# One sequence of 48 units for the cross-attention of a decoder trunk, with the cached keys and values asked for in ScalarE's DMA queue

## What is computed

```python
x = x + einsum('bte,ed->btd', o, w_out)                       # mixer's output
# memory of the prompt: 256 tokens
m = rmsnorm(mem_prompt, g_mem)
k = einsum('bmd,de->bme', m, w_k)        # also an output (new_mem_k_prompt)
v = einsum('bmd,de->bme', m, w_v)        # also an output (new_mem_v_prompt)
# cross attention: 4 heads of 512; prompt uses k, v above, the 8 samples use
# cache_mem_k, cache_mem_v: (1, 8, 256, 4, 512) each, 16.8 MB each
q = einsum('btd,de->bte', rmsnorm(x, g_xattn), w_q)
p = softmax(q k^T * 512**-0.5)
x = x + einsum('btd,de->btd', p v, w_o)
# then SwiGLU with D_FF = 5632 and a last RMSNorm
```

## Time and profile before

| | |
|---|---|
| median of 3 runs | 2031.25 us (2029.52 to 2032.12) |
| the profiled execution, its own time | 2029.23 us |
| its span, first to last instruction | 2027.5 us |
| PE busy over the span | 1868.7 us (92%) |
| DVE, ACT, POOL busy | 1158.9, 763.5, 243.3 us |
| mean granted TensorE clock | 0.969 |
| transferred | 362.42 MB, mean 179 GB/s |

### The profile page before, as it was taken

The page is one execution under the profiler, slowest core; times in us unless marked ns, Lnnn a source line. Parts: engine busy times, 40 slices in busy tenths (PEclk is TensorE's granted clock), DMA queues, the critical chain, the costliest instruction groups (busy, mean ns, idle before and its releaser), DMA issues.

```text
span 2027.5 us, 34488 instructions
## 1 busy us (share of the span) xinstructions
PE 1868.7 (92%) x13799; PEld 1749.6 (86%) x13799; DVE 1158.9 (57%) x1590; ACT 763.5 (38%) x768; POOL 243.3 (12%) x225
## 2 busy tenths in 40 slices
PE   4999999858695999999988999999999999999996
PEld 3999999755694989977764898999999999999996
DVE  5788445473834655555556565666544466665444
ACT  1454554322224343333333234444333344443332
POOL 6000000001711540000000351000000000000331
PEclk9999999889897999999999999999999999999998
DMA  5455555700032545677867366898745789895552
GB/s 158 153 179 166 168 169 186 225 3 11 1 94 84 180 152 168 227 265 265 319 211 274 96 184 184 256 253 238 197 143 172 207 234 246 242 252 148 171 175 95
DMA packets 407132, 362.42 MB, mean 179 GB/s; under 512 B 10975, under 2 KB 373470, under 8 KB 404214
## 3 DMA queue, kind: packets, MB, share of 16 engines
q1 hardware_dynamic: 379686, 336.53, 53.9%
q10 hardware_dynamic: 27392, 25.17, 3.9%
HBM read 345.67 MB, written 16.19 MB: 178 GB/s over the span
## 4 chain that ended last, share of the span: by engine, by line
PE 84%; DVE 8%; issue 3%; ACT 2%; POOL 1%; DMA 1%; DVEq 0%; POOLq 0%; ACTq 0%; SPq 0%
PE ps L419 64%; PE ps L439 9%; PE ps L831 2%; DVE w_lo L403 2%; PE ps L1158 1%; PE ps L1148 1%; PE ps L947 1%; DMA vc<-in_cache_mem_v_dram 1%; PE ps L1047 1%; PE ps L1112 1%; ACT w_hi L396 1%; PE ps L999 1%; DVE cacc L519 0%; DVE Tm L1853 0%; DMA raw<-in_ffn_w_up_dram 0%
## 5 line engine op out<-in xcount | busy, mean ns | idle before, releaser
L396 ACT ACTIVATE w_hi<-raw 128x2048 fp32r<-128x2048 f32 (+1 forms) x289 | 519.9, 1799 | 924.9 <-PE ps L419 784.4
L403 DVE TENSOR_TENSOR w_lo<-raw,w_hi 128x2048 fp32r<-128x2048 f32 (+1 forms) x289 | 629.6, 2179 | 273.4 <-ACT w_hi L396 269.3
L419 PE MATMUL ps<-act_hi,w_lo 128*128 128x264 f32 x2576 | 740.0, 287 | 3.6 <-DVE w_lo L403 1.9
L419 PE MATMUL ps<-act_lo,w_hi 128*128 128x264 f32 x2576 | 732.3, 284 | 0.0
L419 PE MATMUL ps<-act_hi,w_hi 128*128 128x264 f32 x2576 | 731.8, 284 | 0.0
L419 PEld LDWEIGHTS ps<-act_hi,w_lo 128*128 128x128 f32 x2576 | 487.9, 189 | 6.9 <-DVE w_lo L403 6.2
L419 PEld LDWEIGHTS ps<-act_lo,w_hi 128*128 128x128 f32 x2576 | 488.2, 190 | 0.7
L419 PEld LDWEIGHTS ps<-act_hi,w_hi 128*128 128x128 f32 x2576 | 485.5, 188 | 0.0
L419 PE MATMUL ps<-ff_hi,w_lo 128*128 128x264 f32 x704 | 202.0, 287 | 4.3 <-DVE ff_lo L542 4.3
L419 PE MATMUL ps<-ff_hi,w_hi 128*128 128x264 f32 x704 | 201.4, 286 | 0.0
L419 PE MATMUL ps<-ff_lo,w_hi 128*128 128x264 f32 x704 | 200.9, 285 | 0.0
(11 more groups left out here) (365 smaller groups left out, 1944.2 us busy)
## 6 DMA issues: line engine op xcount, KB each, us to landing
raw<-in_w_in_dram SPq DMA_DIRECT2D x56, 1024.0 KB, 6.8
raw<-in_ffn_w_gate_dram SPq DMA_DIRECT2D x44, 1024.0 KB, 5.8
raw<-in_ffn_w_up_dram SPq DMA_DIRECT2D x44, 1024.0 KB, 10.5
raw<-in_ffn_w_down_dram SPq DMA_DIRECT2D x32, 768.0 KB, 4.8
raw<-in_ffn_w_down_dram SPq DMA_DIRECT2D x32, 640.0 KB, 6.1
raw<-in_w_out_dram SPq DMA_DIRECT2D x16, 1024.0 KB, 6.7
raw<-in_xa_w_q_dram SPq DMA_DIRECT2D x16, 1024.0 KB, 6.7
raw<-in_xa_w_k_dram SPq DMA_DIRECT2D x16, 1024.0 KB, 6.3
```

What stands on the lines that cost most here:

```text
L396: act.activation(w_part(ph, w_hi[b]), raw_part(ph, r, half), ACT.Copy)\
L403: dve.tensor_tensor(w_part(ph, w_lo[b]), raw_part(ph, r, half), w_part(ph, w_hi[b]), ALU.subtract)\
L419: mm = pe.matmul(ps[:, acc(ph, u), 0:ph.cols], w[b][:, k, :], v[:, kk + k, 0:ph.cols], start=first and k == 0 and m == 0, stop=last and k ...
```

## The change

All 48 units of `x_q`, `mem_k` and `mem_v` become one written-out sequence, n = 0 to 47, and the attention's steps are placed between units:

- The query is turned per head (after units 4, 10, 18, 26), and `spread_query` and `sample_scores` run from unit 5 to 36, head by head instead of sample by sample.
- Keys are turned after units 20, 24, 28, 32; the prompt's scores come after 22, 26, 30, 34, its shares are turned after 23, 27, 31, 35; the samples' softmax at 37 and 38.
- Sample values 0 to 15 come after units 40 to 47, two each. Values 16 to 31 and all 16 prompt tiles come after unit 47, one prompt tile and one sample value in turn.
- Keys and values come in 64 pieces of 512 KB, asked for by ScalarE (`piece_in`, line 1527 of the kernel after): the first 14 through three buffers in the room of the turned keys, the others through a ring of eight in the room of `x_q`'s operands. SyncE keeps the weight slots and the results.

```diff
-            for n in range(NB):
-                ph = PH["mem_k" if n < 4 else "mem_v"]
-                load(sp, ph, n % 4, 0)
-                if n:
-                    key_turn(n - 1, 2)
-                    key_turn(n - 1, 3)
...
+            for s in range(3):
+                load_slot(s)
+            for m in range(3 * KT):
+                if m % 2 == 1 and m < 46:
+                    load_slot((m + 5) // 2)
+                if m >= 20 and m % 4 == 0:
+                    rows_out((m - 20) // 4)
...
+            def piece_in(p):
+                if p < EARLY_PIECES:
+                    if p >= EARLY:
+                        W(act, "s_dot", p - EARLY + 1 + 2)
+                elif p < EARLY_PIECES + RING:
+                    act.wait_ge(units_done, PH["mem_k"].u0 + UNIT_CREDIT)
+                elif p < NB * XH + RING:
+                    W(act, "s_dot", p - RING + 1 + 2)
+                else:
+                    W(act, "s_o", p - RING - NB * XH + 1)
...
+                act.dma_start(dst[:, :, :], part.rearrange("(m p) d -> p m d", p=P)).then_inc(landed, 16)
...
+            for n in range(3 * KT):
+                split(*unit_at(n + 2))
+                m = n - 1
+                if 5 <= m < KT and nxt < EARLY_PIECES or KT <= m < 37 or m >= 40:
+                    piece_in(nxt)
+                    nxt += 1
+                    if m >= 40 or 22 <= m <= 30 and m % 2 == 0:
+                        piece_in(nxt)
+                        nxt += 1
...
+                if n >= KT and n % 4 == 3:
+                    keep_rows(n % KT // 4, n // (2 * KT))
...
+                if n >= 39:
+                    for v in range(2):
+                        first_values(2 * (n - 39) + v)
+            for v in range(18, NB * XH):
+                first_values(v)
+                if v % 2 == 1 and nxt < PIECES:
+                    piece_in(nxt)
+                    piece_in(nxt + 1)
+                    nxt += 2
```

More of the change, by code:

```diff
@@ L441, in wide_products, with piece_at, unit_at @@
             mm.then_inc(units_done, 1)
+        def piece_at(p):
+            if p < EARLY_PIECES:
+                return early[p % EARLY], ring_landed[RING - 1 - p % EARLY], 16 * (p // EARLY + 1)
+            n = p - EARLY_PIECES
+            used = len(range(RING - 1 - n % RING, EARLY_PIECES, EARLY)) if n % RING >= RING - EARLY else 0
+            return ring[n % RING], ring_landed[n % RING], 16 * (used + n // RING + 1)
+        def unit_at(m):
+            ph = PH[("x_q", "mem_k", "mem_v", "x_o")[m // KT]]
+            return ph, m % KT // 4, m % 4
         def acc(ph, u):
@@ L653, in _, with load_slot @@
             rest("w_out", True)
[L654 to L670, removed]
+            def load_slot(s):
+                ph, i, u = unit_at(2 * s)
+                load(sp, ph, i, u // 2)
@@ L697, in _ @@
[L697 to L713, removed]
+                dst = o["mem_k" if n < 4 else "mem_v"][0, 0].rearrange("(c p) h d -> p c (h d)", p=P)
@@ L1094, in _, with turn_query @@
             pe.wait_ge(acc_free, PH["x_q"].t0 + ACC_CREDIT)
[L1096 to L1101, removed]
+            def turn_query(h):
+                pe.wait_ge(q_halved, h + 1 + 1)
+                if h:
+                    W(pe, "s_dot", (10, 18, 26)[h - 1] - 6 + 1 + 2)
+                for d in range(4):
+                    mm = turn(ps[0:2 * NB, 6, d * P:(d + 1) * P], q_both[:, h, d, :, :].rearrange("p m b -> p (m b)"))
+                mm.then_inc(q_turned, 1)
@@ new lines, in spread_query, with turn_keys @@
+            def spread_query(n):
+                W(pe, "s_dot", n + 1)
+                if n in (0, 6, 14, 22):
+                    pe.wait_ge(q_kept, (0, 6, 14, 22).index(n) + 1)
+                h, b = n // NB, n % NB
+                mm = pe.matmul(ps[:, 6 + n % 2, :], pick_row[:, b:b + 1].broadcast_to([P, P]), q_rows[:, h % 2, :],
+                               start=True, stop=True)
+                mm.then_inc(N["s_qb"], 1)
+            def turn_keys(g):
+                rows_wait(pe, 0, g)
+                if g:
+                    W(pe, "att_pT", g)
+                pe.wait_ge(k_kept, 2 * g + 2)
+                for d in range(4):
+                    for c in range(2):
+                        mm = turn(ps[:, 4 + d // 2, (d % 2) * NM + c * P:(d % 2) * NM + (c + 1) * P],
+                                  vm[:, c, g * XD + d * P:g * XD + (d + 1) * P])
+                mm.then_inc(k_turned, 1)
@@ new lines, in scores, with turn_prompt @@
+            def scores(h):
+                pe.wait_ge(k_kept, 2 * h + 2 + 2)
+                for c in range(NC):
+                    for d in range(4):
+                        mm = pe.matmul(ps[:, 4, c * NM:(c + 1) * NM], q[:, 4 * h + d, c * P:(c + 1) * P],
+                                       kT[:, 4 * h + d, :], start=d == 0, stop=d == 3)
+                mm.then_inc(N["att_qk"], 1)
+            def turn_prompt(h):
+                W(pe, "att_norm", h + 1)
+                for m in range(2):
+                    for c in range(NC):
+                        mm = turn(ps[:, 5, m * T + c * P:m * T + (c + 1) * P], pr[:, h, c * NM + m * P:c * NM + (m + 1) * P])
+                mm.then_inc(N["att_pturned"], 1)
@@ new lines, in turn_sample_scores, with turn_sample_shares, sample_values @@
+            def turn_sample_scores():
+                W(pe, "s_dot", NB * XH + 2)
+                for m in range(2):
+                    mm = turn(ps[0:NB * XH, 7, m * P:(m + 1) * P], sc_s[:, m, :])
+                mm.then_inc(N["s_st"], 1)
+            def turn_sample_shares():
+                W(pe, "s_pn", 1)
+                for m in range(2):
+                    mm = turn(ps[:, 7, NM + m * 32:NM + (m + 1) * 32], p_s[:, m * P:(m + 1) * P])
+                mm.then_inc(N["s_ptt"], 1)
+            def sample_values(n):
+                b, h = n // XH, n % XH
+                pe.wait_ge(v_mixed, n + 1)
+                at = NB * XH - 1 - (NB * h + b)
+                pe.matmul(ps[0:NB * XH, 6, :], window[:, at:at + NB * XH], piece_at(NB * XH + n)[0][:, 0, :],
+                          start=n == 0, stop=n == NB * XH - 1).then_inc(N["s_o"], 1)
@@ new lines, in prompt_values @@
+            def prompt_values(j):
+                if j >= 2:
+                    W(pe, "att_oe", j - 1)
+                for m in range(2):
+                    mm = pe.matmul(ps[:, 4 + j % 2, 0:T], vm[:, m, j * P:(j + 1) * P],
+                                   prT[:, j // 4, m * T:(m + 1) * T], start=m == 0, stop=m == 1)
+                mm.then_inc(N["att_o"], 1)
+            for n in range(3 * KT):
+                ph, i, u = unit_at(n)
+                if n < KT:
+                    pe.wait_ge(m_taken, n + 1)
+                    pe.wait_ge(mt_ready, n + 1)
@@ L1140, in _ @@
[L1140 to L1160, removed]
@@ L1163, in _ @@
[L1163 to L1175, removed]
@@ L1176, in _ @@
[L1176 to L1185, removed]
[L1186 to L1198 removed]
+                else:
+                    if n == KT:
+                        pe.wait_ge(m_taken, KT + 2)
+                    wide_products(pe, ph, i, u)
@@ new lines, in _ @@
+                if n == 38:
+                    turn_sample_shares()
+                if n == 40:
+                    pe.wait_ge(columns_ready, 4)
+                if n >= 40:
+                    for v in range(2):
+                        sample_values(2 * (n - 40) + v)
+            for v in range(2):
+                sample_values(16 + v)
+            W(pe, "att_pT", XH)
+            rows_wait(pe, 1, 3)
+            for j in range(KT):
+                prompt_values(j)
+                if j < 14:
+                    sample_values(18 + j)
@@ L1936, in sample_scores @@
                 ins.then_inc(N["s_dot"], 1)
-                if h == XH - 1:
-                    W(dve, "s_dot", n + 1 + 2)
-                    dve.tensor_copy(sc_s[:, :, XH * b:XH * b + XH], sc_b).then_inc(s_kept, 1)
-            for n in range(2 * KT):
-                if n:
-                    sample_scores(n - 1)
-                if n + 2 < 2 * KT:
-                    split(PH["mem_v" if n + 2 >= KT else "mem_k"], (n + 2) // 4 % 4, (n + 2) % 4)
-                else:
-                    split(PH["x_o"], 0, n + 2 - 2 * KT)
```

277 lines of the change are left out of this document (125 added, 152 removed).

## The result

| | before | after |
|---|---|---|
| median (range), 4 runs each on one chip | 2030.38 us (2028.88 to 2032.12) | 2009.9 us (2008.94 to 2011.94) |
| ratio, with its 95% interval | | 0.99 (0.9883 to 0.9917) |
| profiled execution, own time and span | 2029.23, 2027.5 us | 2009.11, 2007.4 us |
| from `x_q`'s first turn to `x_o`'s first matmul | 384.2 us | 361.5 us |

The kernel is 20.5 us faster by the medians. The prediction said 13.3 us, and its range began at 2012, 2.1 us above the result. All of the gain is in the stretch that the change rewrites, which is 22.7 us shorter. The rest of the span is 1643.3 us before and 1645.9 us after.

What follows compares the result with a forecast made beforehand. TensorE was taken as fully busy in the units, so only the attention's 14.5 us idle and 7.2 us slow clock could go: 21.7 minus 8.4 added gives 13.3 us gain, 2017 us, range 2012 to 2029 (forecast's own 2012 to 2023).

Steps and rivals of the forecast that it cites:

- The stops: TensorE's waits left: 3.3 us behind unit 47, 1.4 at the attention's end, 0.2 for the samples' softmax at units 37 and 38.
- The step behind unit 47: TensorE has values 14 and 15 ready, then waits for value 16 from 1.8 to 5.1 us after unit 47: +3.3 us.
- Query turns: Eight query turns become sixteen, priced from 1.02 us for eight key turns: at most +1.0 us, taken as +0.9.
- Slow clock behind the stop: TensorE's lower clock level after the 3.3 us stop behind unit 47: +2.6 us, ends 0 and 2.9.
- What must stay hidden: Splits, weight slots, pieces and ScalarE's requests beside the units, and written-out `x_q`: all taken to cost 0 on TensorE's path.
- Requests on ScalarE: 64 piece requests at 0.45 us each, ends 0.45 and 2.6, one or two beside a unit; ScalarE late for nothing.
- Written-out `x_q`: 768 matmuls of `x_q`, a loop before, written out: cost taken as 0, ends 0 and 92 us.
- Late values: Sample values behind unit 47 paced by pieces landing: seven pairs lose 0.8 us each, 5.6 us, about 2022 to 2023; chance 0.15.
- stalled requests: Rival 2: requests stall ScalarE 2.6 us each, behind unit 47 gain gone and 4 us lost, about 2034; chance 0.06.
- late slots: Rival 3: weight slots late because pieces share bandwidth; at 200 GB/s 31 us over 21 slots, about 2048; chance 0.06.
- slow instruction supply: Rival 4: written-out `x_q` instructions arrive slower than 0.121 us a matmul; at 0.16, 30 us, about 2047; chance 0.03.
- Rival 1: Values come too late behind unit 47, a pair taking 2.7 to 4.6 us against TensorE's 3.8; chance 0.15.

## Why the prediction was off

The direction was right, and so was the mechanism that was forecast: idle time and slow clock go, a few small stops stay. But half of the gain has another source. By its own steps:

- **The stops.** Forecast 3.3, 1.4 and 0.2 us, measured 3.2, 1.4 and 0.2. The step behind unit 47, worked out from what is queued on ScalarE and VectorE, holds to 0.1 us, and the two kernels without it show its cause: the split that stood ahead of the values.
- **Query turns.** Forecast +0.9, measured +0.9: sixteen take 4 x 0.44 us in the chain where eight took 0.87. That is luck. The 1.02 us of the earlier trace rows belong to eight key turns behind a 32-row spread. The 0.9 allowed for half-wide tiles, but a turn takes 0.11 us in both kernels. The query turns of before stand in another row:

```profile
846.36 0.87 PE ps L831 x8
```

- **Slow clock behind the stop.** Forecast 2.6, measured 3.42 - 1.83 = 1.6 us. The ends 0 and 2.9 held. Of three other kernels with the same stop, one had it (1.6 us) and two had none.
- **The step that failed: "So units cannot get faster by this change; what can go is the attention's waiting and its slow clock."** TensorE was busy all through the units, and from this the prediction took over their rows at their old price ("that is 0.43 us of spreading and 5.78 us of matmuls") without asking whether the diff changes an operand. It does, 32 rows become 128. A spread now takes 0.23 us and a unit behind it 5.59, and 32 spreads at 0.36 are 11.5 us less. The stretch with TensorE busy for 201.47 of 201.47 us held this loss: the profile counts it as work.
- **A second step that failed, the other way: "the other 62.2 us are TensorE's own work at full clock, and the change keeps all of it, only in other places"**, with each piece costing "the same between two units as in a row". It rested on the key turns, in a place where a 32-row spread stood ahead of them and had made them dear already (1.02, of which 0.15 are the spread's). Sample values are still narrow, and the change moves them from rows of eight into alternation with full matmuls: seven units behind pairs at +0.19 and 14 prompt tiles with a value at 2.04 instead of 1.9, +3.3 us.

With these in place the sum nearly closes: -13.3 as forecast, -1.0 for the clock, -11.5 for the spreads, +3.3 for the sample values, together -22.5. Measured 361.5 - 384.2 = -22.7 us. That it agrees so closely is luck, since a single profile's clock alone can move it by 1.5, and small terms are left out: 16 prompt scores, for one, take 3.45 us now and took 3.65 at full clock (1055.05 to 1058.70 in the earlier trace rows).

The clue was in the trace of before. The unit behind a spread took 5.78 us. The same 24 matmuls behind key turns took less, in a row that the earlier trace rows leaves out and the prediction does not use:

```profile
872.86 5.58 PE ps L439 x24
```

The Trainium skill, "TensorEngine Tiling (Array Packing)", section "Key Properties", says that a change of tiling mode drains TensorE. The rows of this case agree with it in kind, about 0.2 us on either side of a matmul that isn't full, and weight loads that no longer run under the matmul ahead; that it is this drain, no trace here shows. The Trainium skill's "TensorE: Matmul & The Clock Gate" says, in its table "Why this matters for your kernels", that a single matmul with K = 32 takes the time of one with K = 128. Between full ones it does not: 0.43 against 0.23 us, and the measurement decides.

- **What must stay hidden.** Splits, weight slots and pieces stayed hidden: ScalarE waited 15.4 us in all for value pieces, TensorE never. Requests on ScalarE took 0.38 us one at a time, and up to 1.9 us for two at the end, beside a running activation. The forecast of 2.6 us a request as upper end was not reached.
- **Written-out `x_q`.** 5.82 us a unit behind its turn, so the written-out instructions cost nothing, as forecast.
- **The rivals.** Late values, stalled requests, late slots and slow instruction supply each had a mark in the profile, and none of the four marks is there. Rival 1 came nearest. ScalarE did wait for value pieces behind unit 47 and took 2.4 us a value there (six of them from 1073.01 to 1087.64), more than TensorE's 2.04. Its lead hid it: the last value was scaled by 1093.7 and summed from 1100.0 on. For the second queue the kernel with all pieces in SyncE's settles it: it neither helps nor harms.

Where the 20.5 us come from, by experiments: the spread's width 10.0 us (2009.9 against 2019.86; by its rows 11.5, of which the profiled executions hide 1.5 in the clock), the new order 10.5 us (2019.86 against 2030.34), the second queue nothing. In the old order the width is worth 14.3 us by the medians and 13.6 in the stretch.

## What to carry to other kernels

Look in the chain of waits for one block of matmuls that has two durations; what stands ahead of the longer one is what makes it so, and a small matmul with fewer than 128 rows or columns between full ones can be worth padding with zeros, which cost one memset on GpSimd here. When a diff touches an operand's shape, price that instruction anew, even where the change is about something else. Behind the last unit of a sequence, work for a later stage (a split for `x_o`) should stand behind what the next matmul waits for, on every engine of the path.

## What was not expected of the hardware

- A matmul over 32 or 64 rows of 128, between full ones, takes 0.43 us instead of 0.23, and what follows takes 0.15 to 0.2 us more (5.78 instead of 5.59 for 24 matmuls, 3.65 instead of 3.45 for 16 scores). With 32 of 128 weight columns it is the same in what follows.
- What the price is in the trace: the weights of a matmul with 32 rows or 32 columns, and those of the full one behind it, are loaded only from the start of their own matmul on, where otherwise they are loaded under the one ahead (884.58 and 885.00 against 879.96 and 880.20 above).
- The same stop of 3.2 to 3.3 us was followed by a slow clock in two profiles and not in two others. Nor does the length of a stop decide it: in the kernel before one of 2.24 us was followed by a granted clock of 0.50 (a prompt tile in 2.05 us), in the same kernel with a 128-row spread one of 2.65 us by a clock of 1.00 (a tile in 1.10 us). The stretch of 3.5 us behind the stop, in the kernel after:

```profile
1069.00:1072.50 3.50, 3.37 (x5) 0.56 (x5) 1.41 (x3) 2.03 (x4) 0.00 (x0) 0.54 0.92 268
```

In the kernel after with 32-row spreads the granted clock is 1.00 over the like stretch, 1079.10 to 1082.60, and ten matmuls run instead of five.

What decides it stays open. Each kernel was profiled once, so it isn't known either whether the kernel after always pays it. Also open is why the weights are loaded late beside a matmul that isn't full.
